# Last attention of a two-block forward pass: value products with loaded values and streamed weights, two heads side by side

## The reference

```python
q, k, v, z = jnp.split(h @ w_in, 4, axis=-1)      # 1024 -> 4 x 1024
q = rms_norm(heads(q), q_gain) * (HEAD_DIM ** -0.5)
k = rms_norm(heads(k), k_gain)
...
s_own = jnp.where(own_dist[None] >= 0,
                  s_own - slopes[:, None, None] * own_dist.astype(jnp.float32)[None], NEG)
...
p = jax.nn.softmax(scores, axis=-1).astype(v.dtype)
...
y = out * jax.nn.silu(z)
return y @ w_out
```

## Time and profile before

| | |
|---|---|
| runs (3) | 1382.88 to 1382.96 us, median 1382.94 us |
| the profiled execution's own time | 1382.92 us |
| its span, first to last instruction | 1381.1 us |
| PE busy | 1371.9 us (99%) |
| DVE busy | 932.0 us (67%) |
| ACT busy | 724.7 us (52%) |
| POOL busy | 121.5 us (9%) |
| bytes moved | 251.42 MB, 182 GB/s over the span |
| granted PE clock | 1.0 of full speed in the whole span |

### The profile page before, as it was taken

How to read it: one execution, slowest core, us unless ns; L and a number is a source line. 1 busy time by engine, 2 the same in 40 slices (tenths; PEclk the granted TensorE clock), 3 DMA queues, 4 the chain that set the end, 5 groups by cost and what they waited for, 6 DMA issues and landing times.

```text
span 1381.1 us, 19736 instructions
## 1 busy us (share of the span) xinstructions
PE 1371.9 (99%) x6916; PEld 1153.8 (84%) x6916; DVE 932.0 (67%) x1112; ACT 724.7 (52%) x991; POOL 121.5 (9%) x161
## 2 busy tenths in 40 slices
PE   8999999999999999999999999999999999999999
PEld 7888888888888888888888888888888888888787
DVE  6777767666667776577777454577775676577675
ACT  6444455445455444475445366654444565545674
POOL 0111010000011110010110010011110110002100
PEclk9999999999999999999999999999999999999999
DMA  8656646556646666447566554455567446555441
GB/s 258 205 182 198 211 146 203 169 190 201 200 129 193 191 211 233 139 152 236 188 199 229 162 193 148 138 164 186 182 206 243 153 163 206 182 171 181 143 132 64
DMA packets 186958, 251.42 MB, mean 182 GB/s; under 512 B 15588, under 2 KB 115724, under 8 KB 186892
## 3 DMA queue, kind: packets, MB, share of 16 engines
q1 hardware_dynamic: 186604, 250.43, 56.0%
q10 hardware_dynamic: 288, 0.13, 0.0%
HBM read 249.45 MB, written 1.05 MB: 181 GB/s over the span
## 4 chain that ended last, share of the span: by engine, by line
PE 92%; DVE 5%; POOL 1%; ACT 1%; issue 1%; DMA 0%; POOLq 0%; DVEq 0%; ACTq 0%
PE sums L519 17%; PE sums L521 17%; PE sums L520 17%; PE sums L667 11%; PE turn L667 11%; PE turn L672 6%; PE sums L672 6%; DVE w_lo L1540 2%; PE turn L597 1%; PE turn L519 1%; PE turn L521 1%; PE turn L520 1%; POOL stat L1016 1%; DVE stat L1985 0%; DVE work L1982 0%
## 5 line engine op out<-in xcount | busy, mean ns | idle before, releaser
L1540 DVE TENSOR_TENSOR w_lo<-raw,w_hi 128x1024 fp32r<-128x1024 f32 x460 | 553.5, 1241 | 147.9 <-ACT w_hi L1087 146.7
L1087 ACT ACTIVATE w_hi<-raw 128x1024 fp32r<-128x1024 f32 x460 | 470.6, 1054 | 237.2 <-DMA raw<-in_ffn_w_up_dram 97.4
L519 PE MATMUL sums<-w_hi,x_both 128*128 128x512 f32 x608 | 242.7, 399 | 0.2 <-issue 0.2
L521 PE MATMUL sums<-w_hi,x_both 128*128 128x512 f32 x608 | 237.2, 390 | 0.0
L520 PE MATMUL sums<-w_lo,x_both 128*128 128x512 f32 x608 | 236.9, 390 | 0.0
L519 PE MATMUL sums<-w_hi,y_hi 128*128 128x512 f32 x510 | 200.3, 393 | 0.0
L521 PE MATMUL sums<-w_hi,y_lo 128*128 128x512 f32 x510 | 198.7, 390 | 0.0
L520 PE MATMUL sums<-w_lo,y_hi 128*128 128x512 f32 x510 | 198.5, 389 | 0.0
L667 PE MATMUL sums<-x_both,w_hi 128*128 128x512 f32 x640 | 160.6, 393 | 0.0
L667 PE MATMUL turn<-x_both,w_hi 128*128 128x512 f32 x640 | 160.3, 392 | 0.0
L519 PEld LDWEIGHTS sums<-w_hi,x_both 128*128 128x128 f32 x608 | 114.2, 188 | 24.5 <-issue 2.3
(11 more groups left out here) (212 smaller groups left out, 1247.4 us busy)
## 6 DMA issues: line engine op xcount, KB each, us to landing
raw<-in_ffn_w_gate_dram SPq DMA_DIRECT2D x176, 256.0 KB, 3.6
raw<-in_ffn_w_up_dram SPq DMA_DIRECT2D x176, 256.0 KB, 4.4
raw<-in_ffn_w_down_dram SPq DMA_DIRECT2D x176, 256.0 KB, 3.7
raw<-in_ret_w_in_dram SPq DMA_DIRECT2D x96, 256.0 KB, 4.1
raw<-in_conv_w_in_dram SPq DMA_DIRECT2D x64, 256.0 KB, 3.9
raw<-in_attn_w_in_dram SPq DMA_DIRECT2D x64, 256.0 KB, 3.9
raw<-in_sb_w_in_dram SPq DMA_DIRECT2D x48, 256.0 KB, 3.5
raw<-in_ret_w_out_dram SPq DMA_DIRECT2D x32, 256.0 KB, 4.1
```

Source lines behind the costliest of these rows:

```text
L519: pe.matmul(bank[:, :], a, wh, start=(first and c == 0), stop=False, skip_group_check=True)
L521: mm = pe.matmul(bank[:, :], b, wh, start=False, stop=(last and c == SC - 1), skip_group_check=True)
L1087: act.activation(w_hi[:, n % RING].rearrange("p c n -> p (c n)"), raw[:, n % RAW].rearrange("p c n -> p (c n)"), ACT.Copy).then_inc(hi_mad ...
L1540: dve.tensor_tensor(w_lo[:, n % RING].rearrange("p c n -> p (c n)"), raw[:, n % RAW].rearrange("p c n -> p (c n)"), w_hi[:, n % RING].rear ...
```

## The change

It swaps the two operands of the value products: the values of a head (128 x 64) are loaded and its transposed weights stream (128 columns). The outputs of the two heads of a pair go to the lower and upper 64 partitions of the same bank, and their products alternate. The result then has head dimensions on the partitions, already in the layout that the output projection needs. So:
- the weights are normalised before their transposition: DVE `mb_norm_p`, at the start of DVE's stage k+1, and `mb_turn_p` on PE waits for it in place of the exponentials;
- `mb_finish` becomes two plain copies for a pair;
- silu(Z) is transposed on PE (`mb_turn_z`) in place of the product, and the gate multiplies in the transposed layout, in four parts, in DVE's stages 6 and 7 and behind stage 9. As the transposed gate lies in a bank that transposed weights use, `mb_turn_p` of heads 11 and 13 waits for the gate product;
- the high and low parts are made from the product in SBUF; silu's second half has a place of its own.

```diff
@@ PE @@
             def mb_turn_p(hd):
-                pe.wait_ge(mb["exp"], 2 * hd + 2)
+                pe.wait_ge(mb["p_normed"], 2 * hd + 2)
...
-                if hd in (13, 15):
-                    pe.wait_ge(y_lo_made, y_base("moba") + (1 if hd == 13 else 2))
+                if hd in (11, 13):
+                    pe.wait_ge(mb["gated"], 1 if hd == 11 else 2)
...
-            def mb_mix(hd):
+            def mb_mix(pair):
...
-                pe.wait_ge(mb["pt_flat"], hd + 1)
+                pe.wait_ge(mb["pt_flat"], 2 * pair + 2)
...
-                pe.matmul(b[:, 0:MDH], work[:, at:at + P], v[:, 0, cols], start=True, stop=True, skip_group_check=True)
-                pe.matmul(b[:, MDH:2 * MDH], work[:, at + P:at + 2 * P], v[:, 0, cols], start=False, stop=False, skip_group_check=True)
-                pe.matmul(b[:, MDH:2 * MDH], work[:, at + 2 * P:at + 3 * P], v[:, 1, cols], start=False, stop=True,
-                          skip_group_check=True).then_inc(mb["o"], 1)
+                for p, kb, q in ((0, 0, 0), (1, 0, 1), (2, 1, 1)):
+                    for e in range(2):
+                        at = MW_HEAD + e * 768 + 384 + p * P
+                        col = ((2 * pair + e) % 8) * MDH
+                        mm = pe.matmul(turn[q][e * MDH:(e + 1) * MDH, 384:512], v[:, kb, col:col + MDH], work[:, at:at + P],
+                                       start=(p < 2), stop=(p != 1), skip_group_check=True)
+                mm.then_inc(mb["o"], 1)
...
-            in_proj("moba_in", 9, hooks, {10: {2: lambda: mb_turn(1, 1)}, 15: {(3, 0): lambda: mb_turn_y(0, 0)}})
+            in_proj("moba_in", 9, hooks, {10: {2: lambda: mb_turn(1, 1)}, 14: {(3, 0): lambda: mb_turn_z(0, 0)},
+                                          15: {(3, 0): lambda: mb_turn_z(0, 1)}})
...
-                     {0: lambda: (mb_turn_y(0, 1), mb_stage(8)), 1: lambda: mb_stage(9),
-                      (3, 0): lambda: mb_turn_y(1, 0), 3: lambda: mb_turn_y(1, 1)})
+                     {0: lambda: mb_stage(8), 1: lambda: mb_stage(9), 2: lambda: (mb_turn_z(1, 0), mb_turn_z(1, 1))})
@@ ACT @@
                     if hd >= 2:
-                        act.wait_ge(mb["o"], hd - 1)
+                        act.wait_ge(mb["o"], hd // 2)
...
             def mb_y_hi(half, i):
-                act.wait_ge(mb["y_turned"], 2 * half + i + 1)
+                act.wait_ge(mb["gated"], 2 * half + i + 1)
@@ DVE @@
-            def mb_finish(hd):
+            def mb_norm_p(hd):
...
                 dve.wait_ge(mb["exp"], 2 * hd + 2)
                 dve.reciprocal(sm[:, 4:6], sm[:, 2:4]).then_inc(mb["recip"], 1)
...
+                    rows = work[:, at + t * P:at + (3 if t else 1) * P]
+                    dve.tensor_scalar(rows, rows, sm[:, 4 + t:5 + t], None, ALU.mult).then_inc(mb["p_normed"], 1)
+
+            def mb_finish(pair):
+
+                dve.wait_ge(mb["turned"], 6 + 2 * (pair // 4))
+                dve.wait_ge(mb["o"], pair + 1)
...
+                    dve.tensor_copy(work[:, at + t * P:at + (t + 1) * P], turn[t][:, 384:512]).then_inc(mb["rows"], 1)
+
+            def mb_gate(half, i):
+
+                dve.wait_ge(mb["rows"], 8 * half + 4 * i + 4)
+                dve.wait_ge(mb["z_turned"], 2 * half + i + 1)
+                dve.tensor_tensor(mb_outputs(half, i), mb_outputs(half, i), mb_z_bank(half, i)[:, :], ALU.mult).then_inc(mb["gated"], 1)
 
             def mb_stage(k):
 
 
-                for hd in range(2 * k - 4, 2 * k - 2) if k >= 2 else ():
-                    mb_finish(hd)
+                for hd in range(2 * k - 2, 2 * k) if 1 <= k <= MH // 2 else ():
+                    mb_norm_p(hd)
+                if k in (6, 7):
+                    mb_gate(0, k - 6)
+                if k >= 2:
+                    mb_finish(k - 2)
```

More of the change, by code:

```diff
@@ L303, in build @@
             "sq", "sq_step", "r", "normed", "turned", "flat", "s", "t", "max", "negmax", "exp",
-            "pt", "pt_flat", "o", "recip", "rows", "silu", "gated", "y_turned")}
+            "pt", "pt_flat", "o", "recip", "p_normed", "rows", "silu", "gated", "z_turned")}
         block = ctx.enter_context(nc.Block())
@@ L353, in mb_values, with mb_z_bank, mb_z, mb_outputs @@
             return rows.rearrange("p (t n) -> p t n", t=2)
-        def mb_y_bank(half, i):
-            return turn[0] if (half, i) == (1, 1) else turn[3]
+        def mb_z_bank(half, i):
+            return turn[2] if (half, i) == (1, 1) else turn[3]
+        def mb_z(half):
+            at = (MW_Z, MW_V)[half]
+            return work[:, at:at + 1024]
+        def mb_outputs(half, i):
+            at = (MW_Q, MW_K)[half] + 512 * i
+            return work[:, at:at + 512]
         def mb_p_bank(hd):
@@ L948, in mb_turn_p @@
                 mm.then_inc(mb["pt"], 1)
-            def mb_mix(hd):
-                half = hd // 8
-                pe.wait_ge(mb["pt_flat"], hd + 1)
+            def mb_mix(pair):
+                half = pair // 4
+                pe.wait_ge(mb["pt_flat"], 2 * pair + 2)
                 pe.wait_ge(act_read, PHASES["moba_in"].act0 + 10 + 2 * half)
-                at = MW_HEAD + (hd % 2) * 768 + 384
+                if pair >= MH // 2 - 2:
+                    pe.wait_ge(mb["t"], MH)
+                    pe.wait_ge(mb["rows"], 2 * pair)
@@ L965, in mb_stage @@
-            def mb_stage(k):
[L968 to L984, removed]
+                for p, kb, q in ((0, 0, 0), (1, 0, 1), (2, 1, 1)):
[4 more added lines that the diff above has]
+                                       start=(p < 2), stop=(p != 1), skip_group_check=True)
@@ new lines, in mb_mix, with mb_turn_z @@
+                mm.then_inc(mb["o"], 1)
+            def mb_stage(k):
+                if k < MH // 2:
+                    mb_scores(2 * k)
+                    mb_scores(2 * k + 1)
+                if 0 <= k - 2 < MH // 2:
+                    mb_mix(k - 2)
+                if 0 <= k - 1 < MH // 2:
+                    mb_turn_p(2 * k - 2)
+                    mb_turn_p(2 * k - 1)
+            def mb_turn_z(half, i):
+                pe.wait_ge(mb["silu"], half + 1)
+                pe.wait_ge(mb["pt_flat"], 16 if half else 10 + 2 * i)
+                if (half, i) == (0, 1):
+                    pe.wait_ge(mb["gated"], 1)
@@ L985, in mb_turn_y @@
                 for c in range(2):
                     for t in range(NT):
[L987 to L990, removed]
+                        mm = pe.transpose(mb_z_bank(half, i)[:, c * SEQ + t * P:c * SEQ + (t + 1) * P],
+                                          mb_z(half)[:, t * 512 + (2 * i + c) * P:t * 512 + (2 * i + c + 1) * P], ident[:, :])
@@ L992, in _ @@
+                mm.then_inc(mb["z_turned"], 1)
             yb4 = y_base("moba")
@@ L1486, in mb_silu @@
                 act.wait_ge(act_read, ph.act0 + 14 + 2 * half)
-                act.activation(work[:, MW_Z:MW_Z + 1024], work[:, MW_Z:MW_Z + 1024], ACT.Silu).then_inc(mb["silu"], 1)
+                act.activation(mb_z(half), mb_z(half), ACT.Silu).then_inc(mb["silu"], 1)
             def mb_y_hi(half, i):
-                act.wait_ge(mb["y_turned"], 2 * half + i + 1)
+                act.wait_ge(mb["gated"], 2 * half + i + 1)
                 act.activation(y_hi[:, 4 * half + 2 * i:4 * half + 2 * i + 2, :],
-                               mb_y_bank(half, i)[:, :].rearrange("p (c t) -> p c t", c=2), ACT.Copy).then_inc(y_hi_made, 1)
+                               mb_outputs(half, i).rearrange("p (c t) -> p c t", c=2), ACT.Copy).then_inc(y_hi_made, 1)
             for m in range(16):
@@ L1503, in _ @@
                     if half:
-                        act.wait_ge(mb["gated"], t + 1)
-                    dst = work[:, MW_Z + t * 512:MW_Z + (t + 1) * 512]
+                        act.wait_ge(mb["o"], 4)
+                    dst = mb_z(half)[:, t * 512:(t + 1) * 512]
                 copy_rows(ph, m, dst)
@@ L1990, in mb_norm @@
                                       ALU.mult).then_inc(mb["normed"], 1)
-            def mb_finish(hd):
-                half = hd // 8
+            def mb_norm_p(hd):
                 sm = soft[:, 6 * (hd % 8):6 * (hd % 8) + 6]
+                at = MW_HEAD + (hd % 2) * 768
                 dve.wait_ge(mb["exp"], 2 * hd + 2)
                 dve.reciprocal(sm[:, 4:6], sm[:, 2:4]).then_inc(mb["recip"], 1)
-                dve.wait_ge(mb["turned"], 6 + 2 * half)
                 dve.wait_ge(mb["recip"], hd + 1)
-                dve.wait_ge(mb["o"], hd + 1)
@@ L2001, in mb_finish @@
                 for t in range(NT):
[L2002 to L2008, removed]
-                for t in range(NT):
-                    y = work[:, (MW_Q, MW_K)[half] + t * 512:(MW_Q, MW_K)[half] + (t + 1) * 512]
-                    dve.wait_ge(mb["silu"], half + 1)
-                    dve.tensor_tensor(y, y, work[:, MW_Z + t * 512:MW_Z + (t + 1) * 512], ALU.mult).then_inc(mb["gated"], 1)
@@ L2014, in mb_stage @@
-            def mb_stage(k):
```

(14 more changed lines are left out.)

2 lines of the change are left out of this document (removed).

## The result

| | before | after |
|---|---|---|
| median of the runs (4 each) | 1382.95 us | 1398.08 us |
| their spread | 1382.88 to 1382.96 | 1397.09 to 1399.33 |
| the profiled execution's own time | 1382.92 us | 1398.73 us |
| its span | 1381.1 us | 1396.9 us |

The changed kernel takes 1.0109 times as long, 95% interval 1.0098 to 1.0121. It is slower, as forecast, by 15.1 us where 10.7 were forecast, and 0.6 us outside the range.

What follows compares the result with a forecast made beforehand. PE, busy 99% of the span, bounds the kernel, with the DVE and ACT loop of 8.11 us fitting under PE's 8.47. The stage terms sum to +10.7 us on 1382.92, giving 1393.6 us, range 1391.0 to 1397.5.

Steps and rivals of the forecast that it cites:

- stage 1, the new wait: Transposes of heads 0 and 1 wait for DVE's scaling, which stands behind slots s0+22 and s0+23: +4.8 us.
- stage 2, ACT's late copies: ACT copies the transposed K later, so its slots and DVE's stage 2 start 3.3 us later: 1.75 us more.
- stages 3 to 5, the loop of DVE and ACT: The loop grows from 8.11 to 8.67 us, over PE's 8.47, losing 0.2 a stage: +0.6 us.
- stage 6, table load and gate: ACT's table load +0.85, mb_turn_p(11) waiting for a gate product +0.6, the loop's 0.2: +1.65 us.
- stage 7: DVE has no slots in stage 6, so PE waits for nothing: -0.5 us.
- stage 8: Head 15's transposes come 8.86 us after mb_turn_p(12), before 5.82, behind ACT's and DVE's work: +3.0 us.
- last pair, to PE's last product: The last pair of heads gives -0.6 us.
- behind PE's last product: After the last pair no part of y is late; nothing was added to the sum.
- PE's own part: Value products in column halves overlap, 0.67 less, a shape change costs 0.10: -0.57 us a pair, -4.6 in all.
- Rival (b): In the value products, the column halves don't overlap: +1.3 us, 1394.9 us; chance 14%.
- rival (a): PE's clock falls after its idle stretches in stages 1 and 8: 1.6 or 3.1 us, 1395.2 to 1396.7; chance 30%.
- Rival (c): At mb_turn_p of stage 1, the waits are covered and PE's gain stays: -4.6 us, 1378.3 us; chance 3%.

Runs made afterwards that it cites:

- the filled one: The changed kernel with products that nobody reads put on PE where it waits, in stages 1, 2, 6 and 8: 1393.81 us, ratio 1.0078.
- the one-half kernel: The gate earlier, with both heads' value products on the lower half of the columns, so the output is not computed: 1386.11 us, ratio 1.0023.
- The last order of work: The gate earlier, with the first and last pairs' transposes and the last pair's products moved later: 1378.73 us, ratio 0.9969.
- the first experiment: The changed kernel with DVE's scaling of the weights moved behind its score work, ahead of the slots: 1382.53 us, ratio 0.9997.
- the gate earlier: The first experiment with mb_turn_z(0, 0) one slot earlier and its gate product at the end of DVE's stage 5: 1381.69 us, ratio 0.9992.
- head by head: The gate earlier, with a pair's six value products in the order of the heads, not alternating: 1383.36 us, ratio 1.0005.
- normalisation alone: The kernel before with weights normalised at the start of DVE's stage k+1, transposes waiting for it, results copied unscaled; products and gate as before: 1398.76 us, ratio 1.0113.

## Why the prediction was right in its waits and wrong in its size

The terms, measured as how much later the second head's transposes start than before, in the kernel with full clock (the filled one), each less the term above it:

| step of the prediction | forecast | measured |
|---|---|---|
| stage 1, the new wait | +4.8 | 1303.19 - 1298.57 = +4.6 |
| stage 2, ACT's late copies | +1.75 | +1.7 |
| stages 3 to 5, the loop of DVE and ACT | +0.6 | +0.2 |
| stage 6, table load and gate | +1.65 | +1.9 |
| stage 7 | -0.5 | -0.5 |
| stage 8 | +3.0 | +2.9 |
| last pair, to PE's last product | -0.6 | -0.4 |
| behind PE's last product | 0 | +0.5 |
| sum | +10.7 | +10.9 |
| the clock (after less the filled one, medians) | 0 | +4.3 |

The sum came out nearer than its terms did: five of them miss by -0.2, -0.4, +0.3, +0.2 and +0.5 us and cancel, so the agreement within 0.2 is partly luck.

- **What bounds it: right.** The loop of DVE and ACT had room only because nothing of DVE's stage k was wanted in PE's stage k.
- **PE's own part: right.** -0.57 a pair forecast, -0.53 measured where no wait hides it, 4.3 for 4.6 in eight pairs. Rival (b), no overlap, is out: the one-half kernel shows what it would look like. The change of shape cost 0.10, as taken from the scores, also for column halves: the last L975 of stage 7 starts 0.20 before the L956 behind it, where a record costs 0.107. By the Trainium skill, "TensorEngine Tiling (Array Packing)", Key Properties, a change of mode drains the engine; a drain is here no more than that 0.10.
- **Stages 3 to 5: too high by 0.4.** The loop is 8.54 where 8.67 was forecast. The reciprocal, start to start, takes 0.19 where I took 0.25 (1301.75 to 1301.94); two of those in a loop are the 0.12.
- **The step that failed: the price of the clock, nothing in the sum and "half of it would be lost, 1.6 or 3.1 us" in rival (a).** The mechanism was named, but its size was too low and it stood outside the sum. I took the slow stretch as 3.1 us, the least that the earlier trace rows showed, and counted one or two. The profiled execution has three, of 6.8, 3.4 and 3.4 us, and they cost 4.9 there, 4.3 by the medians: with that term the sum is 15.0 and the time 1397.9, 0.2 below the measured one. Half of their length would be 6.8; a part of the first lies before PE resumed (1301.4 to 1302.55) and cost nothing. The argument against it, "no stall in mid-kernel shows it", was empty: the kernel before has no wait of PE longer than 0.6 us after its start, so it could not show one. With a stall of 5 us in the forecast itself, the clock belonged in the sum, not in a rival at 30%.
- **Rival (c)** gave 1378.3 for the case that the waits are covered. The last order of work does that and takes 1378.73. Its price was right within 0.4, though partly by luck: 4.3 and not 4.6 from the products, two waits of before covered besides, and 0.5 more at the kernel's end. Its condition is a matter of where instructions stand.

By the Trainium skill, "TensorE: Matmul & The Clock Gate", Why this matters for your kernels, idle gaps over some 3 us between bursts are to be avoided. The gaps of 4.92 and 3.65 us agree with it, and so does the one of 1.88 in stage 2, behind which the clock stayed full; the slow stretch behind 0.91 and 0.80 us in stage 6 is one that this rule would not have told of.

## What to carry to other kernels

When a change moves an instruction ahead of another engine's wait, look in that engine's timeline for idle time between the moment its input is there and the moment its result is wanted, and write it there; here two lines stood behind the slots instead of ahead of them, and that was worth 15.5 us, over three times what the products gained. A forecast stall of several us on PE has to carry its price in clock in the sum; products that nobody reads, put into the stall, keep the clock up and so tell the two apart.

## What the runs showed of the hardware

- **The clock.** After 4.92 us idle PE ran at half speed until 1308.3, 5.7 us after it resumed. A stretch of 3.4 us came behind waits of 0.91 and 0.80 us in one execution, and none in the filled kernel without filling in stage 6, whose waits there were 0.9 and 0.8. In four kernels whose longest wait in these stages is 0.6 to 1.1 us, 0 of 11 (the first experiment), 3 of 11 (the gate earlier), 2 of 11 (head by head) and 1 of 10 runs (one half) had a clock of 0.999 and took 1.5 to 1.8 us more. The kernel before, the filled one and the one with moved transposes never had it, in 50, 5 and 6 runs. So short waits likely bring a slow stretch now and then; none of those runs was profiled, and where it fell isn't shown.
- **Column halves in plain fp32.** The 12 records of a pair start within 0.60 us, those of the two heads some 6 ns apart. To the next shape they take 0.80 us (1314.94 to 1315.74 in the kernel with the earlier gate), where 12 records on the full array took 1.39.
- **The end of the kernel.** From PE's last product to the end of the span were 2.76 us before and 2.77 with normalisation alone, but 3.28 in every kernel with the swap. DVE's timeline at the end of after:

```profile
1392.27 0.69 DVE L2084 TENSOR_TENSOR h<-sums,h 128x512 f32<-128x512 f32 x1 [0.67 <-PE sums L530]
1393.42 0.75 DVE L2084 TENSOR_TENSOR h<-turn,h 128x256 f32<-128x256 f32 x2 [0.46 <-PE turn L548]
```

From one add to the next are 1.15 us, where before there were 0.78 (1376.98 to 1377.76). Counted from PE's last product, though, only the first of the two last adds is late, by 0.37 us; the last one starts 0.06 later than before. Most of the 0.52 lies behind it, in the writes of the output. The DMA view of the last microseconds, before and then after:

```profile
out_dram<-h SPq DMA_DIRECT2D x1, 256.0 KB, 2.0
out_dram<-h SPq DMA_DIRECT2D x2, 128.0 KB, 1.9
```

```profile
q14 instruction: 1, 0.01, 0.4%
...
out_dram<-h SPq DMA_DIRECT2D x1, 256.0 KB, 2.6
out_dram<-h SPq DMA_DIRECT2D x2, 128.0 KB, 2.2
```

After, one packet of an instruction queue falls among these writes, and they take 0.3 to 0.6 us longer to land; before, and with normalisation alone, no such packet is there. No experiment was made on it, so that it delays the add and the writes is not shown; the cause stays open.
